# Sixteen more sample tokens' expert products from gathered rows, and dense products of 176 columns in place of 192

## The reference, cut to what matters

```python
q = (tb @ wq).reshape(PEER_BLOCK, N_PEER_HEADS, 2, D_KEY_HALF)
s = jnp.einsum('thpk,hpnk->thpn', q, subkeys)
s_top, i_top = lax.top_k(s, TOPK)
...
best, sel = lax.top_k(cand, TOPK)
experts = jnp.take_along_axis(cand_idx, sel, axis=-1)
g = jax.nn.softmax(best, axis=-1)
act = jax.nn.gelu(jnp.einsum('td,thkd->thk', tb, u[experts]), approximate=False)
return jnp.einsum('thk,thkd->td', g * act, v[experts])
```

## Time and profile before

| what | value |
|---|---|
| median of 3 runs | 2738.63 us (2736.59 to 2740.75) |
| the profiled execution | 2734.86 us, of which its span is 2733.0 us |
| TensorE busy (matmul) | 2577.0 us, 94% of the span |
| VectorE busy | 1387.0 us, 51% |
| GpSimd busy | 640.2 us, 23% |
| moved by DMA | 885.36 MB, mean 324 GB/s |

### The profile page before, as it was taken

One profiled execution on the slowest core, in us unless ns is written; L12 is line 12 of the kernel. 1 busy time (PEld: TensorE's weight loads), 2 busy tenths in 40 slices (PEclk: granted clock), 3 DMA queues, 4 the chain that ended last, 5 costly groups with the idle time before them and its releaser, 6 DMA issues. The chain is left out here.

```text
span 2733.0 us, 40504 instructions
## 1 busy us (share of the span) xinstructions
PE 2577.0 (94%) x16081; PEld 2150.6 (79%) x16081; DVE 1387.0 (51%) x3099; ACT 458.3 (17%) x1377; POOL 640.2 (23%) x619
## 2 busy tenths in 40 slices
PE   7889987798999999999999999989999999999998
PEld 5564563346499999999999866464999999999998
DVE  2330020122279979995554121223799799945542
ACT  3210020012011125430000010121111254300000
POOL 0005000000004425564332000000044255633320
PEclk9799999999999999999999999999999999999999
DMA  7789969996918989999999696949099899999995
GB/s 243 246 285 284 363 225 406 405 367 249 405 40 344 373 324 378 389 378 409 409 409 358 227 378 223 379 169 347 1 365 373 314 378 388 370 410 409 409 355 173
DMA packets 249145, 885.36 MB, mean 324 GB/s; under 512 B 27402, under 2 KB 34730, under 8 KB 238159
## 3 DMA queue, kind: packets, MB, share of 16 engines
q1 hardware_dynamic: 169390, 606.97, 59.4%
q0 software_dynamic: 79568, 275.81, 26.4%
HBM read 863.33 MB, written 109.08 MB: 356 GB/s over the span
## 5 line engine op out<-in xcount | busy, mean ns | idle before, releaser
L2952 PE MATMUL ps<-xT,front 128*128 128x192 f32 x4096 | 686.6, 327 | 6.4 <-DMA front<-in_peer_uT 6.3
L2952 PEld LDWEIGHTS ps<-xT,front 128*128 128x128 f32 x4096 | 663.2, 190 | 11.8 <-DMA front<-in_peer_uT 10.6
L2980 PE MATMUL ps<-p1e_S,p_qT 128*128 128x192 f32 x2048 | 336.9, 327 | 4.5 <-DMA p_qT<-in_peer_v 4.5
L2980 PE MATMUL ps<-p0e_S,p_qT 128*128 128x192 f32 x2048 | 337.1, 327 | 4.1 <-DMA p_qT<-in_peer_v 4.1
L2980 PEld LDWEIGHTS ps<-p1e_S,p_qT 128*128 128x128 f32 x2048 | 332.5, 190 | 8.3 <-DMA p_qT<-in_peer_v 8.3
L2980 PEld LDWEIGHTS ps<-p0e_S,p_qT 128*128 128x128 f32 x2048 | 332.3, 190 | 8.2 <-DMA p_qT<-in_peer_v 8.0
L2706 DVE CUSTOM_DVE_ANT_0 front<-front,x_tok 128x1024 f32<-128x1024 f32 x256 | 308.8, 1220 | 9.0 <-DMA front<-in_peer_u,p0e_expert 3.7
L2607 POOL DMA_INDIRECT front<-in_peer_u,p0e_expert x128 | 157.4, 1230 | 353.8 <-DVE p0e_dots L2706 171.3
L2607 POOL DMA_INDIRECT front<-in_peer_u,p1e_expert x128 | 157.4, 1230 | 350.2 <-DVE p1e_dots L2706 172.6
L2717 DVE SCALAR_TENSOR_TENSOR h_tok<-front,p1e_dots,h_tok 128x1024 f32<-128x1024 f32 x127 | 163.1, 1284 | 128.6 <-DMA front<-in_peer_v,p1e_expert 127.2
L2717 DVE SCALAR_TENSOR_TENSOR h_tok<-front,p0e_dots,h_tok 128x1024 f32<-128x1024 f32 x127 | 163.0, 1284 | 126.1 <-DMA front<-in_peer_v,p0e_expert 124.8
(11 more groups left out here) (477 smaller groups left out, 2898.6 us busy)
## 6 DMA issues: line engine op xcount, KB each, us to landing
front<-in_peer_uT SPq DMA_DIRECT2D x256, 512.0 KB, 7.1
p_qT<-in_peer_v SPq DMA_DIRECT2D x256, 512.0 KB, 7.3
out_swa_sample<-in_cache_swa_w SPq DMA_DIRECT2D x32, 2040.0 KB, 23.8
e_ring<-in_mla_pages SPq DMA_DIRECT2D x84, 272.0 KB, 4.9
e_ring<-in_swa_kT SPq DMA_DIRECT2D x16, 1024.0 KB, 9.6
e_arena<-in_swa_v SPq DMA_DIRECT2D x16, 1024.0 KB, 14.1
out_swa_sample<-in_cache_swa_w SPq DMA_DIRECT2D x8, 2016.0 KB, 31.1
e_ring<-in_attn_w_in SPq DMA_DIRECT2D x6, 2048.0 KB, 35.0
```

The lines of the kernel that those rows point to most:

```text
L2952: mm = pe.matmul(k.ps[:, SB[i % len(SB)], 0:TD], ur[:, i % NU, c, :], k.xT[:, c, D0:T], start=(c == 0), stop=(c == KC - 1))
L2980: return pe.matmul(k.ps[:, c // 2, c % 2 * TD:(c % 2 + 1) * TD], vr[:, i % NV, c * P:(c + 1) * P], S[:, i, :], start=False, stop=(i == STE ...
```

## The change

The 16 last sample tokens get a third way. Their 16 x 128 dots with u are computed from gathered rows: each of the 128 partitions takes one (token, head) pair, and 16 gathers, one for each of the 16 experts of a head, fetch the rows. These 16 rows are the numbers 76 to 91 of the gathered rows, which are now 272 (`row_of`); their `row_dot` multiplies by `more_x`, the 16 tokens each repeated on 8 partitions. `more_x` and the expert numbers come by two small DMAs on SP's queue at step 70, behind a wait for `chosen` 3 that was made at step 114 before. Step 100 of ACT has a gelu of the new dots; a DMA at step 104 puts them back as 16 tokens by 128 experts; PE transposes them (`turn_more`) and DVE multiplies the gates of these tokens by them before their one-hots are made. So what the last 4 of the 48 groups spread is gate times gelu already: `copy_gates` copies it for all 128 steps, and `weigh` leaves these groups out.

The u steps have 176 columns in place of 192. The v part keeps 192. The wait and gelu of the 128 dots of the gathered prompt tokens move from step 117 to step 127, and the first `row_add` to row 144. The v load of slot 3 waits at step 120 for row 91 to be used.

```diff
-        self.held, self.bank, self.blocks, self.bank_size = [], 0, 0, 36
+        self.held, self.bank, self.blocks, self.bank_size = [], 0, 0, 37
...
+    MORE = 16
+    TU = TD - MORE
+    MORE_AT, MORE_GELU_AT = 76, 100
+    MORE_GROUP = TU // TG
+    ROWS = 2 * HK + MORE
     TAIL = 2 * D
-    EXP_AT, TURN_AT, DOTS_AT, LAST_SPREAD, LAG = 66, 69, 117, 126, 1
+    EXP_AT, TURN_AT, DOTS_AT, LAST_SPREAD, LAG = 66, 69, STEPS - 1, 126, 1
...
+        def row_of(n):
+
+            if n < MORE_AT:
+                return "dot", n
+            if n < MORE_AT + MORE:
+                return "more", n - MORE_AT
+            return ("dot", n - MORE) if n < HK + MORE else ("add", n - HK - MORE)
...
-                if i == VALUES_FROM:
+                if i == TURN_AT + 1:
                     sp.wait_ge(chosen, 3)
+                    sp.dma_start(more_expert[:, :], carried[64 - MORE:64, :].bitcast(I32)).then_inc(more_landed, 16)
+                    sp.dma_start(more_x, k.x[64 - MORE:64, 2, :].unsqueeze(1).to_broadcast([MORE, PEER_H, D])).then_inc(
+                        more_landed, 16)
+                if i == MORE_GELU_AT + NU:
+                    sp.wait_ge(act_ready, 4)
+                    sp.dma_start(carried[0:MORE, :], more_dots[:, :]).then_inc(more_landed, 16)
+                if i == VALUES_FROM + 2 * (NV - 1):
+                    sp.wait_ge(rows_used, MORE_AT + MORE)
...
-            for n in range(2 * HK):
-                table, col = ("peer_u", n) if n < HK else ("peer_v", n - HK)
+            for n in range(ROWS):
+                kind, col = row_of(n)
+                table, numbers = "peer_v" if kind == "add" else "peer_u", more_expert if kind == "more" else expert
+                if n == MORE_AT:
+                    pool.wait_ge(more_landed, 32)
...
+            link(dve.scalar_tensor_tensor(out=halff[0:64, 0, :], in0=IJ[0:64, 2, 0, :], scalar=float(N_KEYS),
+                                          in1=IJ[0:64, 2, 1, :], op0=ALU.mult, op1=ALU.add))
+            dve.tensor_scalar(out=carried[0:64, :].bitcast(I32), in0=halff[0:64, 0, :], scalar1=float(N_EXPERTS * layer),
+                              scalar2=None, op0=ALU.add).then_inc(chosen, 1)
...
+                    if G + 1 == MORE_GROUP:
+                        dve.wait_ge(turned, 3)
+                        link(dve.tensor_tensor(out=T3[:, 2, TU:TD], in0=T3[:, 2, TU:TD], in1=k.ps[:, spread_bank(G + 1), 0:MORE],
+                                               op=ALU.mult))
                     if G + 1 < GROUPS:
                         one_hots(G + 1)
-                    weigh(G)
+                    if G < MORE_GROUP:
+                        weigh(G)
+                    else:
+                        dve.wait_ge(gate_copied, G + 1)
+                        dve.sem_inc(weight_ready, 1)
                     G += 1
...
-                t0, b = TG * G, SPLIT[G]
+                t0, b = TG * G, SPLIT[G] if G < MORE_GROUP else 0
...
+                if i == MORE_GELU_AT:
+                    act.wait_ge(rows_used, MORE_AT + MORE)
+                    act.activation(more_dots[:, :], more_dots[:, :], ACT.Gelu).then_inc(act_ready, 1)
                 if i == DOTS_AT:
-                    act.wait_ge(rows_used, HK)
+                    act.wait_ge(rows_used, HK + MORE)
...
-                    mm = pe.matmul(k.ps[:, SB[i % len(SB)], 0:TD], ur[:, i % NU, c, :], k.xT[:, c, D0:T],
+                    mm = pe.matmul(k.ps[:, SB[i % len(SB)], 0:TU], ur[:, i % NU, c, :], k.xT[:, c, D0:D0 + TU],
...
+            def turn_more():
+                pe.wait_ge(more_landed, 48)
+                pe.wait_ge(weight_ready, MORE_GROUP - len(SPREAD_BANKS) + 1)
+                pe.transpose(k.ps[:, spread_bank(MORE_GROUP), 0:MORE], carried[0:MORE, :], k.ident[0:MORE, 0:MORE]).then_inc(turned, 1)
...
                 while G < groups_by(i):
                     spread_gates(G)
                     G += 1
+                    if G == MORE_GROUP - 1:
+                        turn_more()
```

More of the change, by code:

```diff
@@ L2498, in peer @@
         tmp = pf[:, NV * D:NV * D + NT * TD].rearrange("p (a t) -> p a t", a=NT)
+        more_x = vr[:, NV - 1, :]
         acc = k.h[:, 0, :]
@@ L2533, in gated_cols @@
         def gated_cols(i):
-            return TG * sum(1 for b in SPLIT if b <= i)
+            return min(TU, TG * sum(1 for b in SPLIT if b <= i))
         def spread_bank(G):
@@ L2543, in turned_by @@
         def turned_by(i, part):
-            return 2 + 2 * part + i
+            return 3 + 2 * part + i
+        def row_of(n):
[4 more added lines that the diff above has]
+            return ("dot", n - MORE) if n < HK + MORE else ("add", n - HK - MORE)
         def rows_due(n):
-            per_layer = [len(range(s, 2 * HK, NG)) for s in range(NG)]
+            per_layer = [len(range(s, ROWS, NG)) for s in range(NG)]
             return 16 * (layer * per_layer[n % NG] + n // NG + 1)
@@ L2702, in gates, with row_dot, row_add @@
                                       op=ALU.mult).then_inc(gated, 1)
-            def row_dot(n):
+            def row_dot(n, x, dot):
                 dve.wait_ge(row_landed[n % NG], rows_due(n))
[L2706 to L2713, removed]
+                dve.tensor_tensor_reduce(out=gr[:, n % NG, :], in0=gr[:, n % NG, :], in1=x, scale=1.0,
+                                         scalar=0.0, op0=ALU.mult, op1=ALU.add, accum_out=dot).then_inc(rows_used, 1)
+            def row_add(n, col):
+                dve.wait_ge(row_landed[n % NG], rows_due(n))
+                if col == 0:
+                    dve.tensor_scalar(out=acc, in0=gr[:, n % NG, :], scalar1=dots[:, col:col + 1], scalar2=None,
                                       op0=ALU.mult).then_inc(rows_used, 1)
                 else:
-                    dve.wait_ge(rows_used, HK + n)
-                    dve.scalar_tensor_tensor(out=acc, in0=gr[:, (HK + n) % NG, :], scalar=dots[:, n:n + 1], in1=acc,
+                    dve.wait_ge(rows_used, n)
+                    dve.scalar_tensor_tensor(out=acc, in0=gr[:, n % NG, :], scalar=dots[:, col:col + 1], in1=acc,
                                              op0=ALU.mult, op1=ALU.add).then_inc(rows_used, 1)
@@ L2748, in row @@
                 n, n_rows = n_rows, n_rows + 1
[L2749 to L2755, removed]
+                kind, col = row_of(n)
+                if kind == "dot":
+                    row_dot(n, k.x[:, 0, :], dots[:, col:col + 1])
+                elif kind == "more":
+                    row_dot(n, more_x, more_dots[:, col:col + 1])
+                else:
+                    if col == 0:
+                        dve.wait_ge(act_ready, 5)
+                        link(dve.tensor_tensor(out=dots[:, :], in0=dots[:, :], in1=IJ[:, 0, 2, :], op=ALU.mult))
+                    row_add(n, col)
             for i in range(len(TILES)):
@@ L2775, in _ @@
                     row()
-                dve.sem_inc(chosen, 1)
+                if i == 1:
+                    dve.sem_inc(chosen, 1)
+            link(dve.scalar_tensor_tensor(out=halff[0:64, 0, :], in0=IJ[0:64, 2, 0, :], scalar=float(N_KEYS),
+                                          in1=IJ[0:64, 2, 1, :], op0=ALU.mult, op1=ALU.add))
+            dve.tensor_scalar(out=carried[0:64, :].bitcast(I32), in0=halff[0:64, 0, :], scalar1=float(N_EXPERTS * layer),
+                              scalar2=None, op0=ALU.add).then_inc(chosen, 1)
             gates()
@@ L2794, in _ @@
             assert G == GROUPS
-            for _ in range(2 * HK - n_rows):
+            for _ in range(ROWS - n_rows):
                 row()
             if final is not None:
-                dve.wait_ge(rows_used, 2 * HK)
+                dve.wait_ge(rows_used, ROWS)
                 for part in range(2):
@@ L2833, in gelu @@
                     last = act.activation(tmp[:, i % NT, 0:g], k.ps[:, SB[i % len(SB)], 0:g], ACT.Gelu)
-                if g < TD:
-                    last = act.activation(S[:, i, g:TD], k.ps[:, SB[i % len(SB)], g:TD], ACT.Gelu)
+                if g < TU:
+                    last = act.activation(S[:, i, g:TU], k.ps[:, SB[i % len(SB)], g:TU], ACT.Gelu)
                 last.then_inc(gelu_done, 1)
```

11 lines of the change are left out of this document (8 added, 3 removed).

## The result

The changed kernel took 2715.45 us (median of 4 runs, 2710.97 to 2719.37), the kernel before on the same chip 2739.69 us (2736.59 to 2741.19). The ratio is 0.9909, with a 95% interval of 0.9891 to 0.9928: 24 us faster, by 20 to 30. The profiled execution took 2710.97 us (2734.86 before), its span is 2709.1 us.

What follows compares the result with a forecast made beforehand. The prediction saw TensorE, DMA and VectorE all near their limits; gains of 6.5 us in A and 6.5 in B less 0.9 in C made 12.1 us a layer, 24.2 off 2738.6, so 2714 us, range 2692 to 2733.

Steps and rivals of the forecast that it cites:

- The step: TensorE's u step: 176 columns take 0.150 us a record, so 2.40 us a step in place of 2.60.
- Part A: u steps 0 to 68 of each layer: 6.5 us gained, bounds 3.4 to 14.
- the full stretches: About 100 us of u steps 0 to 68 where loads land only just in time: no gain, at best 1 us.
- my 2161: `gates` in layer 1 would start near 2161 us, after some 6 us of waiting in place of 13.
- my 2356 and 2678: Layer 1: the last `weigh` wait done near 2356 us, the last add behind the loop near 2678 us.
- Part B: u steps 69 to 125, with the spreads: 6.5 us a layer gained, bounds 3 to 11.6.
- my sum: VectorE work leaving u steps 69 to 125, from fewer weighs and cheaper rows: 3.9 us less.
- My check by DMA bytes: From 2240 to 2369 us, 99 blocks at 409 GB/s fill 127 of 129 us, so only the earlier third gains freely.
- Part C: The v steps: 16 more rows lengthen the sharing with v loads, 0.9 us a layer lost.
- the rival: Gathers end last: adds end 28 us behind TensorE at each layer's end, 32 us slower, 2770; chance 0.07.
- The rule of the skill: HBM limit of about 358 GB/s: the 16 gathers cost 23 us a layer, kernel slower by up to 47.
- The waits I took for nothing: New waits, small DMAs, transpose and gate copies on SP, POOL, TensorE and ACT: no cost counted.

Runs made afterwards that it cites:

- experiment 1: Changed kernel with only the 176 columns, without the 16 added rows, their waits and DMAs: 2712.58 us, ratio 0.9916 to the kernel before.
- experiment 2: Changed kernel with the added rows but u products kept at 192 columns: 2739.7 us, ratio 1.001 to the kernel before.
- Experiment 3: Changed kernel loading only half of each u block from step 4 on: 2694.22 us, ratio 0.9852 to the kernel before.
- Experiment 11: Kernel before with ten second rows moved behind the loop and the gathered dots' gelu at step 123: 2737.86 us, ratio 0.9991 to the kernel before.
- experiment 5: Changed kernel with both half u blocks from step 4 and half-length gathered dots from row 57: 2678.37 us, ratio 0.9782 to the kernel before.
- experiment 4: Changed kernel with gathered dots over 512 of 1024 numbers from row 57 on: 2715.41 us, ratio 0.9922 to the kernel before.
- experiment 12: The changed kernel, unaltered, measured again with more executions: 2716.15 us, ratio 0.9925 to the kernel before.
- Experiment 8: Changed kernel with five rows done ahead of `gates` and 24 more rows left for the v part: 2753.09 us, ratio 1.0052 to the kernel before.
- experiment 6: Changed kernel with five rows done ahead of `gates` and left out of later loop turns: 2718.15 us, ratio 0.9924 to the kernel before.

## Why the prediction was right, point by point

**The step.** The chain of waits of the changed kernel, where the earlier trace rows had the other:

```profile
2031.69 8.39 DMA front<-in_peer_uT
2040.13 21.91 PE ps L2999 x144
...
2167.14 0.89 PE ps L3022 x8
2168.04 2.39 PE ps L2999 x16
```

2.39/16 = 0.149 us a record (forecast 0.150). This held, and experiments 1 and 2 show that the columns alone carry the gain.

**Part A.** -6.3 and -5.8 for -6.5. A step of the full window takes 20 x 16/122 = 2.62 us on average, as before. Over all of A the median landing time is 7.5 us, a third of which is 2.50, and in a stretch where every block is awaited TensorE does nine steps in 23.28 us, 0.16 of which is the last record's overhang: 2.57 us a step.

```profile
2070.16 23.28 PE L2999 MATMUL ps<-xT,front 128*128 128x176 f32 x144 [0.98 <-DMA front<-in_peer_uT]
```

```profile
DMA to landing us min/median/max: 3.8/7.5/8.6
```

That -6.3 and -5.8 came so close to -6.5 is in part luck. I had counted 83 us, some 32 steps, as free. By the starts of the steps only 23 (layer 0) and 19 (layer 1) of 68 ran at 2.39 us in the changed kernel; they gave 4.8 and 4.0 us. The rest of the gain came from the full stretches, to which I had given nothing: 35 and 39 steps went from 2.60 to 2.56 us, since before the change TensorE's own 2.60 was just above what the loads allow. Experiment 3 gives A all that TensorE can win once the u blocks are half as large, so that u loads hold A is shown. That full DMA is what makes them slow rests on the windows (8.4 us at 409 GB/s, 4.7 at 344).

**What stands at the end of A.** VectorE's timeline, answering to the earlier trace rows: one of the two new small instructions, `gates`, the last add.

```profile
2143.37 0.29 DVE L2811 TENSOR_SCALAR p1e_carried<-p1e_S 64x128 int32<-64x128 f32 x1
2149.64 0.67 DVE L2723 TENSOR_REDUCE p1e_den<-p1e_best 128x8 f32<-128x128 f32 x3 [5.98 <-ACT p1e_best L2899]
...
2661.15 1.28 DVE L2745 SCALAR_TENSOR_TENSOR h_tok<-front,p1e_dots,h_tok 128x1024 f32<-128x1024 f32 x1 [1.22 <-DMA front<-in_peer_v,p1e_expert]
```

The wait is 5.98 us (forecast 6). The place, 2149.6, is 11 us before my 2161, because that number lacked what layer 0 and the stretch ahead of it had won by then: the first u step of layer 1 began at 1976.4, not 1989.7. With those 13.3 us it is 2148. The same holds for my 2356 and 2678 (2343 and 2665). SP's two DMAs took 0.62 and 0.60 us to issue, not 0.33.

**Part B.** The size was right (-5.7, -6.9 for -6.5), but the step that led to it named only half of the cause. I subtracted from B's old time what leaves VectorE, as if VectorE had set it. Experiment 11 refutes that: relieved of ten rows, the kernel before gained less than 1 us in B, TensorE held it. What my sum does give is the height of VectorE's floor after the change: its busy time in B fell from 185.4 to 181.8 us, by 3.6 (forecast 3.9). The right sum goes down from above: TensorE's own time falls by 57 x 0.20 = 11.4 to 11.6 us, and the idle time of 2.8 us goes with it when nothing else binds, which is 181.0 (experiment 5), but VectorE stops it at 188.3 (experiment 3) and DMA at 188.3 (experiment 4), and the two together at 189.5. So the forecast met the floor's height, not the cause, and that is luck in part. VectorE had next to no idle time in B's second half (20.00 and 19.96 of 20 us in two windows), as I said, and its waits for copied gates in B went from 8.7 to 4.4 us, so 4.3 of them were saved (I took 3). My check by DMA bytes pointed to the second floor, and only the half dots show that it is as high as the first.

**Part C.** +0.3 and +2.1 for +0.9. Experiments 1 and 2 give the rows 1.1 to 3.0 us a layer, with a mean of 1.7, where the same part repeats within 1 us (346.7 and 347.2 in experiment 12): the term was some 0.8 us a layer too small. It stayed small because, as forecast, the adds still ended ahead of TensorE. The last add began at 2661.15 us, at (2661.15 - 2355.5)/126 = 2.43 us each (forecast 2.42), 30 us ahead of the last v step (forecast 27). Experiment 8 shows that the rival bites where I said, once the last add passes TensorE's end.

**The rule of the skill.** The trace disagrees with the HBM limit of about 358 GB/s in the Trainium skill, "DMA: Bandwidth & Descriptors", section "Where 436 GB/s comes from", as a limit for one core; the section works it out as a stack's rate divided by two cores, and this program runs on one: windows of the changed kernel hold 408 and 409 GB/s, C holds 403 over 296 us, and experiment 2 prices the 16 gathers at 1.4 us a layer in C, where the estimate from the page was 23.

**The waits I took for nothing.** POOL was not stopped at gather 76, `turn_more` took 0.23 us and the new multiplication 0.15. SP waited 0.2 us for ACT's gelu of the new dots. One thing was not quite nothing: behind SP's two small DMAs, from the start of u step 71 to that of the next took 3.75 us in the changed kernel (3.73 in layer 0), and 3.28 in experiment 1, which has no such DMAs. B as a whole was no longer for it (189.2 and 189.7 against 189.3 and 189.3), and in sum experiment 2 leaves all of them at nothing in A and B.

## What to carry to other kernels

Before you give a faster engine its gain, look in each stage for the next limit, and for the one behind that: here two stood at the same 188 us, so relieving either showed nothing, and relieving both by a little (ten rows moved from the crowded steps into the idle time behind the loop) showed 4 to 5 us a layer there, of which the next part took back 0.5 to 2. A load queue that runs n steps ahead sets a floor of landing time over n for the step (here 7.5/3 = 2.50 us, with steps of 2.56); where another queue fills DMA, a shorter step does not shorten it. Work put into an engine's wait can cost time when it brings a burst of transfers in front of a bounded stream.

## What the runs showed of the hardware

All 16 DMA engines held 409 GB/s for tens of us, with one queue of gathered 4 KB rows and one of 512 KB blocks; the u queue's share was then a block per 2.6 us. In the burst of experiment 6 the issue of one indirect DMA held POOL for 5.12 us, where the median is 0.94 and the longest in the changed kernel 2.96. I had expected neither that, nor that seven gathers would make two u blocks late in a window whose mean was only 362 GB/s.
